# Two-group encoder step on one core: the first tile's value products in two halves, with the value weights split by halves between the first tile's steps

## What is computed

```python
def rmsnorm(x, w):
    xf = x.astype(jnp.float32)
    y = xf * lax.rsqrt(jnp.mean(xf * xf, axis=-1, keepdims=True) + EPS)
    return (y * w.astype(jnp.float32)).astype(x.dtype)
...
def attn_project(hn, w_in, pos):
    p = hn @ w_in
    q, k, v, z, qi, ki, wi = split_cols(p, [ATT_WIDTH, KV_WIDTH, KV_WIDTH, ATT_WIDTH, IDX_HEADS * IDX_DIM, IDX_DIM, IDX_HEADS])
```

## Time and profile before

| | us |
|---|---|
| median of 3 runs | 1449.46 |
| lowest and highest of them | 1448.16, 1450.64 |
| the profiled execution, its own time | 1447.48 |
| its span, first to last instruction | 1445.6 |
| TensorE busy in the span | 1380.3 (95%) |
| VectorE, ScalarE, GpSimd busy | 904.1 (63%), 641.2 (44%), 674.3 (47%) |

### The profile page before, as it was taken

The page is one execution under the profiler, slowest core; times in us unless marked ns, Lnnn a source line. Parts: engine busy times, 40 slices in busy tenths (PEclk is TensorE's granted clock), DMA queues, the critical chain, the costliest instruction groups (busy, mean ns, idle before and its releaser), DMA issues. The chain is left out here.

```text
span 1445.6 us, 21141 instructions
## 1 busy us (share of the span) xinstructions
PE 1380.3 (95%) x8028; PEld 1202.4 (83%) x8028; DVE 904.1 (63%) x1632; ACT 641.2 (44%) x1123; POOL 674.3 (47%) x469
## 2 busy tenths in 40 slices
PE   5999999999998999989999999999999999997998
PEld 5999845999986555558889999999999999996786
DVE  4211287999995877434558585858585858496232
ACT  4333365678774656531124443434343535253121
POOL 2466700564645766730024464747473738373000
PEclk9999999999999999989999999999999999998999
DMA  6221100223213310002231111111111111105321
GB/s 217 87 64 44 44 1 1 60 76 92 76 56 112 108 29 5 0 30 88 88 93 46 30 36 45 36 45 35 45 36 45 36 45 35 46 6 211 101 88 66
DMA packets 95315, 86.80 MB, mean 60 GB/s; under 512 B 5584, under 2 KB 83280, under 8 KB 95216
## 3 DMA queue, kind: packets, MB, share of 16 engines
q1 hardware_dynamic: 93584, 80.63, 18.2%
q0 software_dynamic: 1632, 4.82, 0.9%
HBM read 65.46 MB, written 19.97 MB: 59 GB/s over the span
## 5 line engine op out<-in xcount | busy, mean ns | idle before, releaser
L187 PE MATMUL bank<-hn_hi,rw_hi 128*128 128x352 f32 x768 | 251.1, 327 | 1.6 <-DVE hn_lo L177 1.6
L187 PE MATMUL bank<-hn_hi,rw_lo 128*128 128x352 f32 x768 | 247.6, 322 | 0.0
L187 PE MATMUL bank<-hn_lo,rw_hi 128*128 128x352 f32 x768 | 247.2, 322 | 0.0
L187 PE MATMUL bank<-hn_hi,w_hi 128*128 128x352 f32 x648 | 210.3, 324 | 3.3 <-ACT relu L676 2.5
L187 PE MATMUL bank<-hn_lo,w_hi 128*128 128x352 f32 x648 | 207.8, 321 | 0.0
L187 PE MATMUL bank<-hn_hi,w_lo 128*128 128x352 f32 x648 | 207.7, 321 | 0.0
L945 POOL TENSOR_SCALAR probs<-probs,low 128x128 f32<-128x128 f32 (+8 forms) x72 | 127.7, 1778 | 62.8 <-DVE low L1080 62.6
L187 PEld LDWEIGHTS bank<-hn_hi,rw_hi 128*128 128x128 f32 x768 | 144.7, 188 | 3.5 <-issue 3.0
L187 PEld LDWEIGHTS bank<-hn_lo,rw_hi 128*128 128x128 f32 x768 | 145.2, 189 | 0.0
L187 PEld LDWEIGHTS bank<-hn_hi,rw_lo 128*128 128x128 f32 x768 | 144.8, 189 | 0.0
L725 POOL TENSOR_TENSOR swapped<-swapped,sin 128x352 f32<-128x352 f32 x57 | 55.4, 971 | 186.4 <-ACT swapped L672 125.8
(11 more groups left out here) (231 smaller groups left out, 2965.3 us busy)
## 6 DMA issues: line engine op xcount, KB each, us to landing
rw_raw<-in_rec_w_in SPq DMA_DIRECT2D x32, 512.0 KB, 4.1
w_raw<-in_att_w_in SPq DMA_DIRECT2D x27, 512.0 KB, 4.0
q_rotated<-relu SPq DMA_DIRECT2D x24, 176.0 KB, 1.9
xin<-in_x_prompt SPq DMA_DIRECT2D x8, 512.0 KB, 4.0
wo_raw<-in_att_w_out SPq DMA_DIRECT2D x4, 1024.0 KB, 8.4
x_again<-in_x_prompt SPq DMA_DIRECT2D x8, 512.0 KB, 4.1
residual<-h_rows SPq DMA_DIRECT2D x8, 512.0 KB, 2.9
wf_raw<-in_rec_w_out SPq DMA_DIRECT2D x4, 1024.0 KB, 9.2
```

The source lines that it names most:

```text
L187: last = pe.matmul(out, l, r, start=n == 0, stop=n == len(passes) - 1)
```

## The change

Four edits, all in `input_norm`. (1) The load of `ident` is issued third, behind the first tokens and the norm weights, in place of first. (2) ScalarE makes the upper part of the first half of the value weights right behind the squares of tile 0, then `upper(0)`, then the second half; squares 1 and 2 follow, and `upper(1)`. (3) VectorE scales tile 0, makes the lower part of the first half of the weights, `hn_lo` of tile 0, the lower part of the second half, and then scales tiles 1 and 2. (4) TensorE's value products are a function of a tile and a half (slices 0 to 3, or 4 to 7), each half with its own waits; the first half of products 0 stands between transposes 0 and transposes 1, the second half behind transposes 1. From t = 2 on the two halves follow each other as before. The number of matmuls, copies and transfers is the same.

```diff
@@ -314,7 +314,6 @@
     KV = KVH * HD
 
     def sync(sp):
-        sp.dma_start(ident[:], io["ident"]).then_inc(ident_in, 16)
         for t in range(NT):
             if t >= 3:
                 sp.wait_ge(xn_ready, t - 2)
@@ -322,6 +321,7 @@
             sp.dma_start(xin[0:rows(t), t % 3, :], token_rows(io, t)).then_inc(x_in[t % 3], 16)
             if t == 0:
                 sp.dma_start(norm_w, io["norm_w"][0].partition_broadcast(P)).then_inc(norm_in, 16)
+                sp.dma_start(ident[:], io["ident"]).then_inc(ident_in, 16)
                 for g in range(2):
                     ks = slice(4 * g, 4 * g + 4)
                     sp.dma_start(wv_raw[:, ks, 0:KV], w_in[:, ks, V0:V0 + KV]).then_inc(wv_in[g], 16)
@@ -350,6 +350,11 @@
                 act.wait_ge(tr_ready, 2 * t + g + 1)
                 act.copy(S["hn_hi"][:, 4 * g:4 * g + 4, span(t)], transposed(t, g)).then_inc(hi_done, 1)
 
+        def value_weights(g):
+            ks = slice(4 * g, 4 * g + 4)
+            act.wait_ge(wv_in[g], 32)
+            act.copy(wv_hi[:, ks, :], wv_raw[:, ks, :]).then_inc(wv_hi_done, 1)
+
         def read_v(t):
             act.wait_ge(v_ready, t + 1)
             src = wide[token_block(t)[1], 2 + t % 2, :]
@@ -363,13 +368,12 @@
                 act.wait_ge(squares_ready, t)
             act.activation(junk[0:r], xin[0:r, t % 3, :], ACT.Square,
                            accum_out=stats[0:r, 0, t:t + 1]).then_inc(squares_ready, 1)
-            if t >= 1:
+            if t == 0:
+                value_weights(0)
+                upper(0)
+                value_weights(1)
+            if t >= 2:
                 upper(t - 1)
-            if t == 1:
-                for g in range(2):
-                    ks = slice(4 * g, 4 * g + 4)
-                    act.wait_ge(wv_in[g], 32)
-                    act.copy(wv_hi[:, ks, :], wv_raw[:, ks, :]).then_inc(wv_hi_done, 1)
             if t >= 3:
                 read_v(t - 3)
             if 0 <= t - FIRST_WEIGHT - 2 < W_SLOTS:
@@ -395,27 +399,44 @@
             dve.scalar_tensor_tensor(xn[0:r, t % 2, :], xin[0:r, t % 3, :], stats[0:r, 2, t:t + 1],
                                      norm_w[0:r], ALU.mult, ALU.mult).then_inc(xn_ready, 1)
 
-        dve.wait_ge(norm_in, 16)
-        scale(0)
-        for t in range(NT):
-            if t + 1 < NT:
-                scale(t + 1)
+        def lower(t):
             for g in range(2):
                 dve.wait_ge(hi_done, 2 * t + g + 1)
                 at = slice(4 * g, 4 * g + 4)
                 dve.tensor_tensor(S["hn_lo"][:, at, span(t)], transposed(t, g),
                                   S["hn_hi"][:, at, span(t)].bitcast(F32), ALU.subtract).then_inc(lo_done, 1)
-            if t == 0:
-                for g in range(2):
-                    ks = slice(4 * g, 4 * g + 4)
-                    dve.wait_ge(wv_hi_done, g + 1)
-                    dve.tensor_tensor(wv_lo[:, ks, :], wv_raw[:, ks, :], wv_hi[:, ks, :].bitcast(F32),
-                                      ALU.subtract).then_inc(wv_lo_done, 1)
+
+        def value_weights(g):
+            ks = slice(4 * g, 4 * g + 4)
+            dve.wait_ge(wv_hi_done, g + 1)
+            dve.tensor_tensor(wv_lo[:, ks, :], wv_raw[:, ks, :], wv_hi[:, ks, :].bitcast(F32),
+                              ALU.subtract).then_inc(wv_lo_done, 1)
+
+        dve.wait_ge(norm_in, 16)
+        scale(0)
+        value_weights(0)
+        lower(0)
+        value_weights(1)
+        scale(1)
+        for t in range(1, NT):
+            if t + 1 < NT:
+                scale(t + 1)
+            lower(t)
             if t == 4:
                 dve.wait_ge(columns_ready, 1)
                 dve.tensor_copy(columns[:].rearrange("p l k -> p (l k)"), wide[:, 0, 0:4 * KT]).then_inc(columns_out, 1)
 
     def tensor(pe):
+        def values(t, g):
+            pe.wait_ge(lo_done, 2 * t + g + 1)
+            pe.wait_ge(wv_lo_done, g + 1)
+            for k in range(4 * g, 4 * g + 4):
+                for x, w in ((S["hn_hi"], wv_hi), (S["hn_hi"], wv_lo), (S["hn_lo"], wv_hi)):
+                    last = pe.matmul(wide[:, 2 + t % 2, 0:VW], x[:, k, token_block(t)[0]], w[:, k, :],
+                                     start=k == 0 and x is S["hn_hi"] and w is wv_hi,
+                                     stop=k == KT - 1 and x is S["hn_lo"])
+            return last
+
         pe.wait_ge(ident_in, 16)
         for t in range(NT + 1):
             if t < NT:
@@ -432,16 +453,15 @@
             if t == 4:
                 pe.wait_ge(rows_in, 48)
                 pe.transpose(wide[:, 0, 0:4 * KT], by_row[:], ident[0:4 * KT, 0:4 * KT]).then_inc(columns_ready, 1)
-            if t >= 1:
-                m = t - 1
-                pe.wait_ge(lo_done, 2 * m + 2)
-                if m == 0:
-                    pe.wait_ge(wv_lo_done, 2)
-                if m >= 2:
-                    pe.wait_ge(v_read, m - 1)
-                product(pe, wide[:, 2 + m % 2, 0:VW],
-                        [lambda k, x=x: x[:, k, token_block(m)[0]] for x in (S["hn_hi"], S["hn_lo"])],
-                        [lambda k, x=x: x[:, k, :] for x in (wv_hi, wv_lo)]).then_inc(v_ready, 1)
+            if t == 0:
+                values(0, 0)
+            elif t == 1:
+                values(0, 1).then_inc(v_ready, 1)
+            else:
+                if t >= 3:
+                    pe.wait_ge(v_read, t - 2)
+                values(t - 1, 0)
+                values(t - 1, 1).then_inc(v_ready, 1)
 
     return dict(sync=sync, tensor=tensor, scalar=scalar, gpsimd=gpsimd, vector=vector)
 
```

## The result

The changed kernel takes 1439.99 us (median of 5 runs, 1437.41 to 1443.88) where the kernel before takes 1449.46 (5 runs, 1447.53 to 1450.64): 9.5 us faster, a ratio of 0.9942 with a 95% interval of 0.9921 to 0.9963. The ratios here are of means, so this one is 8.4 us, within 5.4 to 11.5. I had forecast 3.9 us, and a time between 1443.0 and 1448.9. The profiled execution took 1437.41 of its own, against 1447.48 before.

What follows compares the result with a forecast made beforehand. TensorE's work plus idle spots bound the kernel; only the first stage changes. Order and pause give 4.0 us, with the clock's rise 3.9: median 1449.46 - 3.9 = 1445.6 us, range 1443.0 to 1448.9.

Steps and rivals of the forecast that it cites:

- Where the work goes: First stage: half product from 11.8, tile 1 scaled from 14.3, first weight cast from 9.0, transposes 2 at 20.4 us.
- The 4.0 us of order and pause: Transposes 2 at 20.4, not 24.41: 1.66 of pause less 0.3 delay, plus 12 matmuls x 0.22.
- the clock's lag: Time from TensorE's start after a pause to the rise to 2.4 GHz: 3.4 to 5.7 us, 5.2 taken.
- R: Moment the clock rises in the first stage: 19.1 to 21.4 us, taken as 20.9, counted from unbroken work at 15.65.
- My formula: Gain at the first stage = 4.1 - 0.44 x (R - 20.4) us; 3.9 at the forecast rise.
- rival B: First stage: clock rises right behind the first half product, before transposes 1; gain 6.2 us, time 1443.3; chance 0.12.
- What TensorE wins before 20 us, everything behind it inherits.: Behind the first stage TensorE hardly stops, so the gain made there carries through; forecast gain 3.9 us.
- A: First stage: only products count towards the clock's rise and the halves are too short; gain 1.2, time 1448.3; chance 0.28.
- C: Clock misses products 1 too and rises within products 2; slower, 1451.0 to 1452.0 us; chance 0.05.
- D: TensorE waits out its 4 us before 50 us for a token load or tables; gain 0, 1449.5; chance 0.07.
- Within 0.2%: Whole kernel: total not distinguishable from no change, within about 2.9 us; chance 0.45, against faster 0.52, slower 0.03.
- the line of 2.9: Whole kernel: about 0.2%, what a measurement can tell from no change; a total under 1446.6 us counts as faster.

Runs made afterwards that it cites:

- f_ident_first: The changed kernel with the load of ident issued first, as before the change; 1440.46 us, ratio 0.9947 to the kernel before.
- fill_after: The changed kernel with idle matmuls (ident by ident) put on TensorE into its later pauses; 1433.58 us, ratio 0.9899 to the kernel before.
- best: fill_after with fewer idle matmuls: 6 for 14 ahead of the output product, 3 for 6 and 6 for 10 around the last block; 1435.37 us.
- g_whole_wait: The changed kernel, but from tile 1 on the products wait for both groups of hn_lo, as before; 1437.74 us, ratio 0.9924.
- a_pe_old: The changed kernel with TensorE's old order, weights and queue as changed; 1441.75 us, ratio 0.9954; second profile's run 1442.67 us.
- stage_fill: The changed kernel with 10 idle matmuls in the first stage, around transposes 0 and behind the half product; 1439.55 us, ratio 0.9922.
- best2: best with the same 10 idle matmuls in the first stage as stage_fill; 1434.43 us, ratio 0.9886 to the kernel before.
- b_fill_mm: The kernel before with 10 useless float32 matmuls of ident by ident between transposes 0 and 1; 1442.65 us, ratio 0.9964.
- c_fill_tr: The kernel before with 20 useless transposes of ident between transposes 0 and 1; 1443.28 us, ratio 0.9968.
- e_pe_new: The kernel before with the changed kernel's TensorE order alone; ScalarE, VectorE and the queue as before; 1444.89 us, ratio 0.9976.
- fill_before: The kernel before with 86 idle matmuls (ident by ident) put on TensorE into its five later pauses; 1441.52 us, ratio 0.9950.

## Why the prediction was wrong

**Where the work goes** was right to 0.1 us for the half product, to 0.15 for tile 1's scaling and to 0.3 for ScalarE's casts (the first starts at 8.70, forecast 9.0). The 4.0 us of order and pause are tested by f_ident_first, where the clock rose late and transposes 2 stood at 19.88: 4.5 us ahead of before. The 0.5 more is 0.17 of the earlier scaling and 0.35 of a misreading. I let the second half start when the 1.97 us of transposes 1 end, but their last end is modelled: the next product starts 17.10 - 15.48 = 1.62 behind their start.

The forecast of 3.9 falls short of the 10.1 of the profiled pair in three places: 2.8 us up to transposes 3, of which 0.44 x (20.9 - 14.5) - 0.4 = 2.4 is the clock; 0.5 at the products of tile 7; and 2.9 behind the stage.

**The step that failed in the stage is the clock's lag.** I wrote "with products 0 (5.7) the bounds of the lag are 3.4 and 5.7" and "if all of this counts, R is 19.1 to 21.4". Three starts of one trace were taken as the whole range, and the 2.8 us half product behind a pause was ruled out for being "under every lag seen". R was 14.5, 2.8 us after the half product began. My formula then gives 4.1 + 0.44 x (20.4 - 14.5) = 6.7, less 0.4 for the idle time between 14.5 and 15.5, in which a high clock gains nothing: 6.3, where the trace has 6.7 at transposes 3. The formula was sound, the R put into it was not. This is rival B, to which I gave 0.12. Of six profiles with these 12 products in the gap and no filling in the stage, three have the early rise (both of the changed kernel, fill_after) and three the late one (best, f_ident_first, g_whole_wait): in hindsight it deserved about a half. The late ones rose 3.6 to 5.5 us behind the start of transposes 1, within my bounds. With six products in the gap both profiles are late, with none both of a_pe_old.

Three of six against none of four could be chance, so that the half product brings the early rise isn't shown by these alone. The other orders point the same way. Leaving out stage_fill and best2, which work ahead of transposes 0 too, there are nine profiles with 2.8 us or more of any TensorE work in the gap: five rise before transposes 1 (b_fill_mm and c_fill_tr also), four don't (e_pe_new also). Of the six with less or none, none does. What decides between early and late for the same kernel stays open.

**A term left out:** the halves' own waits from tile 1 on, which I took to change nothing "since the two halves follow each other". They save 0.6 us at the products of tile 7.

**The second step that failed, and the larger one for the total:** "What TensorE wins before 20 us, everything behind it inherits." I put what the rest of the kernel would add at nothing. f_ident_first has the late rise that I had forecast, and is still 8.1 us faster than before (1448.59 on its chip), not 3.9. Each later pause brings its own stretch of low clock, of 3.4 to 13.6 us, whose length doesn't depend on the pause alone, and useless work of c_fill_tr moved the total by 5 us for 1 us of stage. In the profiled pair 2.9 us of the 10.1 came behind the stage: 1.6 by the second low stretch, 0.3 and 0.5 by two shorter waits (for the first queries and for the sample's rows), 0.4 spread. That the low stretches carry part of the surplus is also shown by the filled pair, down to 7.9 from 9.5, and it isn't a matter of one profile. The record has the mean granted clock of each execution, in which the low time ahead of the first rise counts as high: 0.9856 on average over 35 executions of before, 0.9876 over 9 of the changed kernel. A mean clock higher by 0.002 is 0.002 x 2 x 1445 = 5.8 us less time at half the clock, worth at most 2.9 us (an estimate, from values given to 0.001). Why the kernel before has more of it than the variants isn't settled, nor why its waits are longer.

**Rivals:** A's mechanism fell with c_fill_tr; C's (a rise in products 2 or later) occurred in no profile; D didn't occur, the loads kept up. "Within 0.2%" had 0.45 and "faster" 0.52, for a change whose part from order and pause alone, 4.0 us by the sum and 4.5 in f_ident_first, was beyond the line of 2.9; the range ended at B's time without room for a gain behind the stage. The measured 1439.99 lies 3.0 us under it.

## What to carry to other kernels

Work moved into a pause of TensorE is worth more than its own length when it also brings the clock up for what follows. Cost both the early and the late rise, and don't rule one out because a few starts of one trace didn't show it. Before ranking two versions of a kernel by totals a few microseconds apart, compare where the same instruction starts in both traces, stage by stage: low-clock stretches behind later pauses move by more than the edit is worth. And where such pauses can't be removed, a few idle matmuls in them pay (fill_before, 7 us without any other edit), here also where they outlast the pause: cutting 14 to 6 (best) brought nothing measurable.

## What the runs showed of the hardware

- Transposes alone bring the clock up: high within 3.4 us of the start of transposes 0 (8.57) in c_fill_tr, where TensorE had done nothing else.
- A half product of 2.8 us behind a pause of 1.3 to 1.8 us was followed by the rise before transposes 1 in three profiles (at 14.5, 14.9 and 14.9) and not in three others (18.7, 18.9 and 21.0). The changed kernel, f_ident_first and g_whole_wait do the same work up to there.
- The clock fell again over the 2.5 us of pause ahead of products 0, in c_fill_tr just as they began (18.8), in b_fill_mm 1.0 us after (19.7, products from 18.70). So a fall can hit work that is already running.
- The granted clock of the page reads 1.00 until its first change. Ahead of that the spacing of the matmuls has to be read: 0.22 against 0.12 us, as up to 24.7 in before.
